# Turning the input in five banks, splitting it straight from them, and scaling rows from the input itself

## The reference

```python
def rmsnorm(x, g):
    xf = x.astype(jnp.float32)
    y = xf * lax.rsqrt(jnp.mean(xf * xf, axis=-1, keepdims=True) + EPS)
    return (y * g.astype(jnp.float32)).astype(x.dtype)
...
def even_layer(x, g_norm, w_in, conv_w, b_if, g_head, w_pool, s_pool, w_out):
    bsz, s_len, _ = x.shape
    xn = rmsnorm(x, g_norm)
    p = xn @ w_in
    q, k, v, o, z_a, gates, u, z_b = _split(p, EVEN_SPLITS)
```

## Time and profile before

| what | us |
| --- | --- |
| median of 3 runs | 2021.54 (2020.46 to 2022.73) |
| the profiled execution, its own time | 2020.66 |
| its span in the trace | 2018.6 |
| TensorE busy within the span | 1966.1 |

### The profile page before, as it was taken

How to read it: one execution, slowest core, us unless ns; L and a number is a source line. 1 busy time by engine, 2 the same in 40 slices (tenths; PEclk the granted TensorE clock), 3 DMA queues, 4 the chain that set the end, 5 groups by cost and what they waited for, 6 DMA issues and landing times.

```text
span 2018.6 us, 25199 instructions
## 1 busy us (share of the span) xinstructions
PE 1966.1 (97%) x9682; PEld 1505.8 (75%) x9682; DVE 1067.9 (53%) x2013; ACT 772.1 (38%) x1393; POOL 317.9 (16%) x400
## 2 busy tenths in 40 slices
PE   6999999999999899999999999999999999999998
PEld 5787777888757557757788888877766788888886
DVE  5467643444569775485544443343588654444332
ACT  4333433432324463474322222232566442222222
POOL 2450000001000471042000000121155310000000
PEclk8999999999999999999999999999999999999999
DMA  7452334443422222322333333257100133333332
GB/s 176 138 164 68 85 102 146 146 136 83 106 63 63 64 63 84 94 53 64 94 94 94 94 92 96 87 130 218 43 2 2 38 99 94 94 94 94 90 90 71
DMA packets 316781, 187.14 MB, mean 93 GB/s; under 512 B 33519, under 2 KB 297199, under 8 KB 316406
## 3 DMA queue, kind: packets, MB, share of 16 engines
q1 hardware_dynamic: 310254, 168.62, 29.6%
q10 hardware_dynamic: 6408, 16.91, 2.2%
HBM read 183.27 MB, written 17.96 MB: 100 GB/s over the span
## 4 chain that ended last, share of the span: by engine, by line
PE 90%; DVE 5%; ACT 2%; issue 1%; DMA 1%; POOL 0%; ACTq 0%; SPq 0%; DVEq 0%
PE banks L271 23%; PE banks L273 23%; PE banks L272 23%; PE banks L1811 3%; PE banks L1842 3%; PE banks L1825 2%; PE banks L369 2%; PE banks L370 2%; PE banks L371 2%; PE banks L830 1%; PE banks L838 1%; PE banks L928 1%; PE banks L1273 1%; DVE prob L1879 1%; DMA cmp_w<-in_b_cmp_w 0%
## 5 line engine op out<-in xcount | busy, mean ns | idle before, releaser
L271 PE MATMUL banks<-xs,wlo 128*128 128x512 f32 x1336 | 539.7, 404 | 2.2 <-DVE wlo L2187 2.2
L272 PE MATMUL banks<-xs,whi 128*128 128x512 f32 x1336 | 528.9, 396 | 0.0
L273 PE MATMUL banks<-xs,whi 128*128 128x512 f32 x1336 | 528.8, 396 | 0.0
L2187 DVE TENSOR_TENSOR wlo<-raw,whi 128x1024 fp32r<-128x1024 f32 (+1 forms) x283 | 360.1, 1273 | 309.2 <-ACT whi L2178 308.8
L2178 ACT ACTIVATE whi<-raw 128x1024 fp32r<-128x1024 f32 (+1 forms) x283 | 293.5, 1038 | 229.6 <-PE banks L273 164.1
L271 PEld LDWEIGHTS banks<-xs,wlo 128*128 128x128 f32 x1336 | 251.4, 188 | 73.0 <-issue 10.9
L272 PEld LDWEIGHTS banks<-xs,whi 128*128 128x128 f32 x1336 | 251.5, 188 | 61.8 <-issue 3.4
L273 PEld LDWEIGHTS banks<-xs,whi 128*128 128x128 f32 x1336 | 251.4, 188 | 60.8
L463 POOL TENSOR_TENSOR squares<-squares,x_tmp 128x512 f32<-128x512 f32 x35 | 46.8, 1337 | 733.6 <-ACT x_tmp L455 733.6
L271 PE MATMUL banks<-a_hi,wlo 128*128 128x512 f32 x352 | 139.8, 397 | 0.0
L273 PE MATMUL banks<-a_hi,whi 128*128 128x512 f32 x352 | 139.4, 396 | 0.0
(11 more groups left out here) (378 smaller groups left out, 2852.9 us busy)
## 6 DMA issues: line engine op xcount, KB each, us to landing
raw<-in_ffn_w_gu SPq DMA_DIRECT2D x88, 512.0 KB, 3.8
raw<-in_e_w_in SPq DMA_DIRECT2D x56, 512.0 KB, 3.9
raw<-in_ffn_w_down SPq DMA_DIRECT2D x32, 512.0 KB, 4.0
s_skew<-s_bias ACTq DMA_DIRECT2D x6, 2560.0 KB
raw<-in_o_w_in SPq DMA_DIRECT2D x21, 512.0 KB, 4.0
raw<-in_e_w_out SPq DMA_DIRECT2D x16, 512.0 KB, 3.9
raw<-in_b_w_in SPq DMA_DIRECT2D x15, 512.0 KB, 4.3
raw<-in_ffn_w_down SPq DMA_DIRECT2D x16, 384.0 KB, 3.4
```

What stands on the lines that cost most here:

```text
L271: nc.tensor.matmul(out, k.wlo[:, chunk.slot, at, :], self.x_hi(kt), start=first, stop=False)
L272: nc.tensor.matmul(out, k.whi[:, chunk.slot, at, :], self.x_lo(kt), start=False, stop=False)
L273: ins = nc.tensor.matmul(out, k.whi[:, chunk.slot, at, :], self.x_hi(kt), start=False, stop=last)
L2187: self.nc.vector.tensor_tensor(self.wlo[:, chunk.slot, 0:chunk.blocks, :], self.raw[:, chunk.slot, 0:chunk.blocks, :], hi.bitcast(F32), AL ...
```

## The change

The input is turned into five banks (3 to 7) in turn instead of two. The high part and the low part of each tile are made straight from the bank, and the copies to `hT` follow behind: three of them between the low parts 4 to 6, five after all. After the turn of tile 4 TensorE puts in the products of tile 0 of `e_u` with the first four input tiles (`lead=4`), then turns tiles 5 to 7. Chunk 0 is issued ahead of the input's right half. ScalarE starts with a one-element square, and makes the squares of the input from its rows (eight instructions that add up along the row, L427) after splitting chunk 1; GpSimd has no part in it. The scale (`EnterScale`) is made as a column scale of 4 values a partition first (L446, L448, L441, L450), and TensorE turns it into `rb` by four products (L435), which VectorE copies (L452). This happens after tile 1 instead of tile 0 (`scale_at=1`); tile 0 is taken out there too.

```diff
--- before.py
+++ after.py
@@ class Dense @@
-                 between=None, evict_first=False, lead=0, trail=None):
+                 between=None, evict_first=False, lead=0, trail=None, second=True, scale_at=0):
+        self.second, self.scale_at = second, scale_at
...
+    def evict_due(self, eng, who, n):
+
+        for i in range(0 if n == self.scale_at else n, n + 1):
+            if n >= self.scale_at:
+                self.evict(eng, who, i)
...
@@ on_dve (on_act alike) @@
-                if n == 0 and self.scale is not None:
+                if n == self.scale_at and self.scale is not None:
                     self.scale.dve(dve)
                 if n == 0 and self.evicted is not None:
                     self.evicted(dve)
-                self.evict(dve, "dve", n)
+                self.evict_due(dve, "dve", n)
...
@@ on_pe @@
         if self.lead:
-            self.enter(pe, first + 1)
-            self.products(pe, first + 1, 0, 0, 1, range(self.lead))
-            for n in range(2):
-                self.products(pe, first + n, 0, 0, n, range(self.lead, self.sizes[0])).then_inc(summed.sem, 1)
+            if self.second:
+                self.enter(pe, first + 1)
+                self.products(pe, first + 1, 0, 0, 1, range(self.lead))
+            for n in range(2 if self.second else 1):
+                self.products(pe, first, 0, 0, n, range(self.lead, self.sizes[0])).then_inc(summed.sem, 1)
                 for b in self.beside:
                     b.pe(pe, n)
-            first += 2
+                first += 1
...
-                    if n == 0 and self.scale is not None:
+                    if n == self.scale_at and self.scale is not None:
                         self.scale.pe(pe)
...
-class RowScales(RowScale):
+class EnterScale:
...
+    def squares(self, act):
+        for n in range(2 * QT):
+            half, t = divmod(n, QT)
+            if n >= 2:
+                act.wait_ge(self.squared.sem, n - 1)
+            self.k.nc.scalar.activation(self.k.xtmp[:, n % 2, :], self.xin[:, t, 512 * half:512 * half + 512], ACT.Square,
+                                        accum_out=self.parts[:, half, t:t + 1]).then_inc(self.squared.sem, 1)
 
     def pe(self, pe):
-        super().pe(pe)
         k = self.k
         self.free(pe)
+        self.wait_columns(pe)
         for t in range(QT):
-            ins = k.nc.tensor.matmul(k.ps[4][:, t:t + 1], k.squares[:, t * P:(t + 1) * P], k.ones[:, 0:1], start=True, stop=True)
+            ins = k.nc.tensor.transpose(k.ps[SUM_BANK][:, t * P:(t + 1) * P], self.columns[:, t:t + 1].broadcast_to([P, P]),
+                                        k.ident[:, :])
         ins.then_inc(self.turned.sem, 1)
...
+        dve.wait_ge(self.squared.sem, 2 * QT)
+        k.nc.vector.tensor_tensor(self.columns[:, :], self.parts[:, 0, :], self.parts[:, 1, :], ALU.add).then_inc(step.sem, 1)
+        dve.wait_ge(step.sem, 1)
+        k.nc.vector.tensor_scalar(self.columns[:, :], self.columns[:, :], 1.0 / DM, EPS, ALU.mult, ALU.add).then_inc(step.sem, 1)
+        dve.wait_ge(step.sem, 3)
+        k.nc.vector.reciprocal(self.columns[:, :], self.columns[:, :]).then_inc(step.sem, 1)
+        dve.wait_ge(self.turned.sem, 1)
+        k.nc.vector.tensor_copy(k.rb[:, :], k.ps[SUM_BANK]).then_inc(self.kept.sem, 1)
...
@@ class Enter @@
+    def bank(self, m):
+        return self.k.banks[:, 3 + m % 5, :]
...
         for m in range(MT):
             if m % 4 == 0:
                 self.arrived(pe, m // 4)
-            if m >= 2:
-                pe.wait_ge(self.kept.sem, self.kept.at(m - 1))
+            if m == 5:
+                self.first.lead_in(pe)
+            if m >= 5:
+                pe.wait_ge(self.kept.sem, self.kept.at(m - 4))
...
-        for m in range(MT):
-            dve.wait_ge(self.turned.sem, self.turned.at(m + 1))
-            k.nc.vector.tensor_copy(k.hT[:, m, :], k.banks[:, 4 + m % 2, :]).then_inc(self.kept.sem, 1)
-            if m >= 1:
-                low(m - 1)
-            if m == 5:
-                k.split_low(dve, 0)
-        low(MT - 1)
+        def keep(m):
+            k.nc.vector.tensor_copy(k.hT[:, m, :], self.bank(m)).then_inc(self.kept.sem, 1)
+        for m in range(4):
+            low(m)
+        k.split_low(dve, 0)
+        for m in range(3):
+            keep(m)
+            low(4 + m)
+        low(7)
         k.split_low(dve, 1)
+        for m in range(3, MT):
+            keep(m)
...
+        k.nc.scalar.activation(k.xtmp[:, 0, 0:1], k.ones[:, 0:1], ACT.Square)
         self.arrived(act, 2)
         for m in range(MT):
-            act.wait_ge(self.kept.sem, self.kept.at(m + 1))
-            k.nc.scalar.activation(k.xs_hi[:, m, :], k.hT[:, m, :], ACT.Copy,
-                                   scale=k.gains[:, 0, m:m + 1]).then_inc(self.high.sem, 1)
...
+            act.wait_ge(self.turned.sem, self.turned.at(m + 1))
+            k.nc.scalar.activation(k.xs_hi[:, m, :], self.bank(m), ACT.Copy, scale=k.gains[:, 0, m:m + 1]).then_inc(self.high.sem, 1)
+            if m == 3:
                 k.split_high(act, 0)
         k.split_high(act, 1)
-
-    def on_pool(self, pool):
...
+        self.scale.squares(act)
...
@@ even @@
-            e_u = Dense(self, "e_u", xh, xl, self.keep(lambda n: u[:, n, :]), ready=enter.ready, scale=scales,
-                        beside=(tables_beside,))
...
+            e_u = enter.first = Dense(self, "e_u", xh, xl, self.keep(lambda n: u[:, n, :]), ready=enter.ready, scale=scales,
+                                      beside=(tables_beside,), lead=4, second=False, scale_at=1)
...
                     gains.on_sp(sp)
+                    self.load_chunk(sp, 0)
                     x_loads[1].on_sp(sp)
-                    for i in range(SLOTS):
+                    for i in range(1, SLOTS):
                         self.load_chunk(sp, i)
```

More of the change, by code:

```diff
@@ L402, in dve, with __init__ @@
         dve.wait_ge(self.inv.sem, self.inv.at(1))
-class RowScales(RowScale):
[L408 to L411, removed]
+class EnterScale:
+    def __init__(self, k, xin, parts, columns, free):
+        self.k, self.xin, self.parts, self.columns, self.free = k, xin, parts, columns, free
+        self.squared, self.step = k.sig("input_squared"), k.sig("column_scale")
+        self.turned, self.kept = k.sig("scale_turned"), k.sig("scale_kept")
+    def squares(self, act):
[5 more added lines that the diff above has]
+                                        accum_out=self.parts[:, half, t:t + 1]).then_inc(self.squared.sem, 1)
@@ L421, in act @@
     def act(self, act):
[L422 to L425, removed]
+        act.wait_ge(self.step.sem, 2)
+        self.k.nc.scalar.activation(self.columns[:, :], self.columns[:, :], ACT.Sqrt).then_inc(self.step.sem, 1)
     def dve(self, dve):
-        super().dve(dve)
-        k = self.k
-        dve.wait_ge(self.turned.sem, self.turned.at(1))
@@ L431, in dve @@
-        k.nc.vector.tensor_scalar(self.columns[:, :], k.ps[4][:, 0:QT], 1.0 / DM, EPS, ALU.mult, ALU.add).then_inc(self.step.sem, 1)
-        dve.wait_ge(self.step.sem, self.step.at(2))
-        k.nc.vector.reciprocal(self.columns[:, :], self.columns[:, :]).then_inc(self.step.sem, 1)
+        k, step = self.k, self.step
+        dve.wait_ge(self.squared.sem, 2 * QT)
+        k.nc.vector.tensor_tensor(self.columns[:, :], self.parts[:, 0, :], self.parts[:, 1, :], ALU.add).then_inc(step.sem, 1)
+        dve.wait_ge(step.sem, 1)
@@ L599, in __init__ @@
     def __init__(self, k, xin, arrived):
-        self.k, self.xin, self.arrived = k, xin, arrived
+        self.k, self.xin, self.arrived, self.first, self.scale = k, xin, arrived, None, None
         self.turned, self.kept = k.sig("x_turned").take(MT), k.sig("x_kept").take(MT)
         self.high, self.low = k.sig("x_high").take(MT), k.sig("x_low").take(MT)
-        self.made, self.added = k.sig("squares_made").take(MT), k.sig("squares_added").take(MT - 1)
-    def all_added(self):
-        return self.added.at(MT - 1)
+    def bank(self, m):
+        return self.k.banks[:, 3 + m % 5, :]
     def ready(self, pe, m):
@@ L615, in on_pe @@
                 self.arrived(pe, m // 4)
-            if m >= 2:
-                pe.wait_ge(self.kept.sem, self.kept.at(m - 1))
+            if m == 5:
+                self.first.lead_in(pe)
+            if m >= 5:
+                pe.wait_ge(self.kept.sem, self.kept.at(m - 4))
             for t in range(QT):
-                ins = k.nc.tensor.transpose(k.banks[:, 4 + m % 2, t * P:(t + 1) * P], self.xin[:, t, m * P:(m + 1) * P],
-                                            k.ident[:, :])
+                ins = k.nc.tensor.transpose(self.bank(m)[:, t * P:(t + 1) * P], self.xin[:, t, m * P:(m + 1) * P], k.ident[:, :])
             ins.then_inc(self.turned.sem, 1)
@@ L651, in on_act @@
-            if m == 4:
+            act.wait_ge(self.turned.sem, self.turned.at(m + 1))
```

(6 more changed lines are left out.)

14 lines of the change are left out of this document (6 added, 8 removed).

## The result

The changed kernel takes 2030.23 us (median of 5 runs, 2028.64 to 2032.58) against 2021.32 us (2020.39 to 2022.73) for the kernel before: ratio 1.0045, 95% interval 1.0035 to 1.0056. It is slower by 8.9 us, 7 to 11 us by the interval. The profiled execution has a span of 2026.9 us, 8.3 us over that of before.

The account below looks back on a forecast made before the run. TensorE was taken to bound the kernel; tile 2 would begin at 47.45 instead of 39.36, plus 0.2 for half clock, 8.3 us later. Median forecast 2021.54 + 8.3 = 2029.8 us, range 2025.0 to 2033.0.

Parts of the forecast that it names:

- three signs of being wrong: Chunk 3 issued well before 36.96; L435 before chunk 3's low part; or TensorE's waits behind 50 us shrinking correspondingly.
- the end of the wait: TensorE, after tile 1, waits for the column scale behind chunk 3's low part and goes on at 44.35 us.
- the clock: Half clock on the scale's turns, bias pair and start of tile 2: 0.49 + 0.81 + 0.2 = 1.5 us.
- The early part: Input turns through tile 1: tile 1 ends near 33 instead of 38.18, about 5 us earlier, range 31 to 37.
- The squares by row: Eight ScalarE squares, 0.61 to 2.56 us each, hidden before chunk 3 comes unless beyond 1.7 us each.
- The turns of the scale: Four TensorE turns behind the wait for the column scale: 1.1 us, ending at 45.45.
- The bias pair: Bias pair and its second part before tile 2: 1.99 us at half clock, ending at 47.45.
- The turns and the clock: Skill's rule that turns do not count for the clock: half a microsecond more at the scale's turns, 8.8 for 8.3.
- the far end: Upper end of the shift, 9.2 us, if all three half-clock terms ran long.
- Nothing given back later: TensorE's later waits, the mask's 5.5 us the longest, swallow none of the 8.3 us.
- second rival: Scale comes in time but tile 3 still needs chunk 3's low part: gain capped at 2.8 us, 2018.7; chance 0.06.
- The opening claim: TensorE is busy 1966.1 of 2018.6 us, so its idle time, 52.5 us, is all that could be won.

Follow-up runs that it names:

- the run with the scale first: Changed kernel with the scale ahead of the split of chunk 3 on ScalarE and VectorE: 2018.54 us against 2020.86 for the kernel before, ratio 0.9987.
- the run with chunk 3 early: Changed kernel with SyncE issuing chunk 3 ahead of the layer's small tables, VectorE's order unchanged: 2020.4 us against 2020.86 for the kernel before, ratio 0.9996.
- the plain-product run: Changed kernel with the four turns of the scale issued as ordinary products with the identity: 2032.42 us in one run.
- the last version: Changed kernel with scale ahead of chunk 3, chunk 3 ahead of small tables, chunks 1 and 2 split sooner, input tile 2 copied sooner: 2015.57 us against 2021.12.

## Why the prediction was right

The direction, the mechanism and the size hold: 8.3 us were forecast and 8.3 us lie between the two spans, 8.9 between the medians, and the run with the scale first and the run with chunk 3 early each take away one of its two conditions and the loss with it. One of its three signs of being wrong came true: chunk 3 was issued at 34.91, 2 us ahead of 36.96. Two terms were off by over 1 us each, the end of the wait and the clock, and they cancelled; that part of the agreement is luck. By its steps:
- The early part. Forecast about 5 us earlier, tile 1 ending at 33; measured 34.2, some 4 us earlier. The first 12 products took half a microsecond more, since the clock stayed at half for all but the last of them, and the last turn, waiting for its bank (1.7 us), and the other 12 half a microsecond more again. A part of the gain is on VectorE: it made the low part of chunk 0 in 1.23 us instead of 2.28 and each low part of the input in 0.75, where the kernel before took 0.74 at 15.37 and 1.15 or more from 16.63 on. GpSimd was adding squares there from 15.80 on, and has no work there in the changed kernel. No run has this alone.
- The end of the wait. Forecast 44.35, measured 43.15. The steps behind chunk 3 were right (from 42.27, the end of its low part, to 43.15, 0.88 us, against 0.83), but chunk 3 came at 39.96 instead of 41.20, since SyncE issued it 2 us sooner; I had taken one execution's time for fixed. TensorE stood for 8.89 us, not 11, since tile 1 also ended 1.2 us later than forecast.
- The squares by row: 0.62 us and 0.19 for reading each sum, which was not forecast as an instruction of its own; all hidden, as forecast.
- The turns of the scale: forecast 1.1, measured 1.08. The bias pair: forecast 1.99, measured 2.24 (44.16 to 46.40).
- The clock. This term was mis-sized. I had 1.5 us in all, with full clock back soon after tile 2 began; it was back at 49.13, and the loss against the run with the scale first is 1.5 us up to tile 2 and 1.3 in it, 2.8 together. That is 1.3 too little, 1.1 of it in tile 2, for which I had 0.2, and it happened to make good the 1.2 by which the wait ended early. With chunk 3 as late as forecast the sum would have been 9.5 or 9.6, beyond the 9.2 that I had set as the far end without a working.
- The turns and the clock. The Trainium skill, "TensorE: Matmul & The Clock Gate", section "Part 4: PE-mode transpose", by which turns do not count for the clock, gave 8.8. I wrote that the trace does not settle this, which was a misreading. In the kernel before TensorE did nothing but turns up to 23.41. Its first ones, from 10.12, took 0.42 us each, the last of the first sixteen 0.27, and the four of the fifth tile, at 15.60, took 0.63 together, which is full clock. In three more of the ten traces these four are at full clock too (the row at the top of the plain-product run is one), in the other six at half. So the clock does rise behind turns alone, and the trace disagrees with the page. Whether turns count for as much as products is not shown. The 0.5 us by which the rule moved the sum is less than the spread of the clock between executions.
- Nothing given back later by a wait: TensorE is idle for 12.3 us between 50 and 700 us in both traces (650.00 - 637.73), and the waits of over 1 us behind tile 3 are the same, row by row. But the clock moves the difference about. It is 8.4 us at tile 3 and still 8.4 where TensorE has waited 2.55 us for ScalarE (595.33 in the earlier trace rows, 603.70 below), 6.8 at the mask, and 8.3 over the whole span. The products behind the wait of 2.55 us were at half clock from 597 to 600 in the kernel before, and at full clock in the changed kernel, with the same work; later the changed kernel had such a stretch alone (granted clock 0.66 from 1458 to 1463 us, 1.00 for the same work in the kernel before). So that the spans differ by just what tile 3 does is in part chance as well.

The cap of 2.8 us in the second rival was nearly what the run with the scale first gives (2.6 in the trace, 2.3 in the medians). The opening claim that TensorE's idle time is all that could be won was too narrow: in the last version the span is 6.6 us shorter, and only half of that is idle time; TensorE is busy for 1962.8 us instead of 1966.1, of which the two sums of squares that are gone are 1.65.

The wait of 2.55 us in the changed kernel, and the mask's in the kernel before and in the changed one:

```profile
603.70 1.03 PE L1290 MATMUL banks<-zT,member 128*16 128x512 f32 x2 [2.55 <-ACT zT L1283]
```

```profile
675.11 1.19 PE L1808 MATMUL banks<-mask,ident_r 128*128 128x512 f32 x2 [5.53 <-DVE mask L1095]
```

```profile
681.92 1.19 PE L1825 MATMUL banks<-mask,ident_r 128*128 128x512 f32 x2 [5.54 <-DVE mask L1112]
```

Stretches of TensorE (start:end, length, busy, granted clock, DMA share, GB/s), kernel before and changed kernel:

```profile
50.00:700.00 650.00, 637.73 (x2728) 0.99 0.35 106
```

```profile
50.00:700.00 650.00, 637.73 (x2704) 0.99 0.35 106
```

## What to carry to other kernels

When work is pulled forward, look at what stands ahead of each new wait on the engine that feeds it: here a few 4-column instructions stood behind a split of weights, and the split behind a transfer that had to pass all small tables. A transfer that is late without harm becomes a bound as soon as something urgent is queued behind its reader. Order each queue by when its result is wanted, and only then count what a faster start is worth.

## What was not expected of the hardware

Idle products in a wait did not keep the clock up: with 36 of them and a gap of 0.81 us, TensorE was at half clock from 45.5 to 48.5 us, after the gap and not in it. Waits of 0.81 and 1.94 us in other runs left it at full. The half clock behind the first product lasted 3.5 us in the kernel before and 5.7 with one transfer moved; with the changed kernel's instructions it lasted 5 us in one execution and 2 in another. So a clock loss read from one execution is good to 1 or 2 us here, no better. And turns alone, with no product before them, were followed by full clock in four of ten executions (0.63 us for four turns, against 1.09 to 1.12 at half).
